# A decoder trunk on one core: the first loads of V's gated weights issued in U's tail, and V's first products formed ahead of U's last chunk

## What is computed

```python
q = (xf @ wq).reshape(n, PEER_HEADS, 2, PEER_DK // 2)
s = jnp.einsum('nhpd,hpkd->nhpk', q, keys)
...                       # top 16 of each head's candidates: experts (128 per row) and gate
hi = jax.nn.gelu(jnp.einsum('bed,bd->be', jnp.take(u_tab, ei, axis=0), xi))
return jnp.einsum('be,bed->bd', gi * hi, jnp.take(v_tab, ei, axis=0))
```

## Time and profile before

| | us |
|---|---|
| median of 3 runs | 3460.92 (3460.67 to 3470.65) |
| the profiled execution, its own time | 3460.77 |
| its span in the trace | 3458.7 |

### The profile page before, as it was taken

One profiled execution on the slowest core, in us unless ns is written; L12 is line 12 of the kernel. 1 busy time (PEld: TensorE's weight loads), 2 busy tenths in 40 slices (PEclk: granted clock), 3 DMA queues, 4 the chain that ended last, 5 costly groups with the idle time before them and its releaser, 6 DMA issues.

```text
span 3458.7 us, 54628 instructions
## 1 busy us (share of the span) xinstructions
PE 3294.1 (95%) x19630; PEld 3118.4 (90%) x19630; DVE 2473.4 (72%) x5134; ACT 1463.5 (42%) x2581; POOL 876.3 (25%) x690
## 2 busy tenths in 40 slices
PE   8998989999999979999998898999999997999998
PEld 7833589999999979999998788999999997999997
DVE  3243268878788868888873327888788877888886
ACT  3222243356666623333333314346666652333333
POOL 3211010000045443334431001000015543343441
PEclk9988999999999989999999879999999998999999
DMA  4254523455599999999972112356569999999994
GB/s 142 97 158 117 160 75 102 141 201 180 204 339 372 364 381 366 360 362 363 361 268 63 48 47 77 105 162 213 180 208 380 382 358 360 369 355 371 355 370 146
DMA packets 315826, 835.34 MB, mean 242 GB/s; under 512 B 32248, under 2 KB 155256, under 8 KB 311440
## 3 DMA queue, kind: packets, MB, share of 16 engines
q1 hardware_dynamic: 233472, 541.63, 44.7%
q0 software_dynamic: 82192, 291.85, 23.2%
HBM read 726.25 MB, written 107.11 MB: 241 GB/s over the span
## 4 chain that ended last, share of the span: by engine, by line
PE 91%; DVE 3%; ACT 2%; DMA 2%; issue 1%; SPq 0%; POOLq 0%; ACTq 0%; POOL 0%; DVEq 0%
PE pstr L1634 30%; PE aux L1711 16%; PE pstr L1711 16%; PE pstr L1423 14%; PE aux L1669 5%; PE pstr L1545 2%; PE pstr L1565 1%; PE aux L1454 1%; PE aux L1463 1%; DMA hl<-hidden 1%; PE aux L1624 1%; PE pstr L1518 1%; PE aux L1765 1%; PE aux L1764 1%; DVE rstd L979 0%
## 5 line engine op out<-in xcount | busy, mean ns | idle before, releaser
L946 DVE TENSOR_TENSOR wlo<-wraw,whi 128x1024 fp32r<-128x1024 f32 x600 | 734.2, 1224 | 589.3 <-ACT whi L680 588.0
L680 ACT ACTIVATE whi<-wraw 128x1024 fp32r<-128x1024 f32 x600 | 632.6, 1055 | 319.8 <-PE pstr L1711 237.5
L1634 PE MATMUL pstr<-xh,whi 128*128 128x392 f32 x2048 | 719.9, 352 | 0.0
L1634 PE MATMUL pstr<-xl,whi 128*128 128x392 f32 x2048 | 699.0, 341 | 0.0
L1634 PE MATMUL pstr<-xh,wlo 128*128 128x392 f32 x2048 | 697.8, 341 | 0.0
L653 POOL DMA_INDIRECT rows<-in_ur,idx x256 | 364.5, 1424 | 1306.2 <-DVE hs L1181 750.8
L653 POOL DMA_INDIRECT rows<-in_v,idx x256 | 378.1, 1477 | 550.1 <-DVE ysum L1194 461.3
L1711 PE MATMUL aux<-wth,whi 128*128 128x392 f32 x1024 | 351.1, 343 | 42.8 <-DVE wtl L1241 42.8
L1634 PEld LDWEIGHTS pstr<-xl,whi 128*128 128x128 f32 x2048 | 386.6, 189 | 0.0
L1634 PEld LDWEIGHTS pstr<-xh,whi 128*128 128x128 f32 x2048 | 386.3, 189 | 0.1
L1634 PEld LDWEIGHTS pstr<-xh,wlo 128*128 128x128 f32 x2048 | 386.2, 189 | 0.0
(11 more groups left out here) (240 smaller groups left out, 5282.0 us busy)
## 6 DMA issues: line engine op xcount, KB each, us to landing
wraw<-in_u SPq DMA_DIRECT2D x256, 512.0 KB, 4.0
wraw<-in_v SPq DMA_DIRECT2D x256, 512.0 KB, 6.4
hidden<-hid SPq DMA_DIRECT2D x256, 196.0 KB, 3.8
gates<-gst SPq DMA_DIRECT2D x28, 1792.0 KB, 9.2
gc<-gates SPq DMA_DIRECT2D x64, 784.0 KB, 10.0
hl<-hidden SPq DMA_DIRECT2D x256, 196.0 KB, 6.6
wraw<-in_w SPq DMA_DIRECT2D x88, 512.0 KB, 3.5
kv<-in_ck SPq DMA_DIRECT2D x32, 256.0 KB, 3.1
```

The costliest lines, as they stand in the source:

```text
L680: e.activation(whi[:, s % RING, :], wraw[:, s % RING, :], ACT.Copy).then_inc(w_hi, 1)
L946: e.tensor_tensor(wlo[:, s % RING, :], wraw[:, s % RING, :], whi[:, s % RING, :].bitcast(F32), ALU.subtract).then_inc(w_lo, 1)
L1634: mm = e.matmul(pstr[:, r % 2, 0, 0:ND], w[:, r, k * P:(k + 1) * P], x[:, k, 0:ND], start=k == 0 and w is whi and x is xh, stop=k == KB - ...
```

## The change

Three things are done.

1. The tiles get other homes. `gc` becomes two tiles that lie over the two buffers of `gst`; `wth` and `wt` lie over the ranking's `tv` and `ti`; `wtl` takes the place over `xt` where `wt` was. None of them lies over the one-hots any more.
2. SyncE issues the first loads inside U's loop: `hl` 0 and 1 behind `store_h(120)`, the first half of the gates behind block 13's store (after a wait for the even blocks), `hl` 2 and 3 behind `store_h(122)`, the second half behind `store_h(123)` (after a wait for the odd blocks, block 13 among them).
3. `gated(0)`, `gated(1)` and `split_wt(0)` on VectorE stand ahead of the split of V's chunk 3 and of the dots of U's chunk 127. `round_wt(0)` on ScalarE stands ahead of `take_hidden(127)`.

No instruction and no transfer is added or taken away.

```diff
-        wt = place("wt", [P, 2, ND], F32, at_xt + 8192)
+        wtl = place("wtl", [P, RING, ND], F32R, at_xt + 8192)
...
+        at_top = used[0]
         tv = place("tv", [P, NT, NPAIR, TOPK], F32)
...
-        used[0] = at_rank
-        gc = place("gc", [P, 2, NB, CPL, SPAN_T], F32)
-        wth = place("wth", [P, RING, ND], F32R)
-        wtl = place("wtl", [P, RING, ND], F32R)
+        gc = [place(f"gc{n}", [P, NB, CPL, SPAN_T], F32, at_gst + n * P * SPAN_T * 4) for n in range(2)]
+        wth = place("wth", [P, RING, ND], F32R, at_top)
+        wt = place("wt", [P, 2, ND], F32, at_top + RING * ND * 4)
...
                             if c == group_slot((b + 1) * BLOCK - 1) + 1:
                                 store_gates(b)
-                for par in range(2):
-                    e.wait_ge(gates_out[par], 16 * (NB // 2) * (layer + 1))
-                load_gates(0, 0)
-                load_gates(0, 1)
-                for c in range(RING):
-                    load_h(c)
+                        if c == G_END - 1:
+                            e.wait_ge(pick_ready, (layer + 1) * (NT - 1))
+                            load_h(0)
+                            load_h(1)
+                        if c == G_END:
+                            e.wait_ge(gates_out[0], 16 * (NB // 2) * (layer + 1))
+                            load_gates(0, 0)
+                        if c == G_END + 1:
+                            load_h(2)
+                            load_h(3)
+                        if c == G_END + 2:
+                            e.wait_ge(gates_out[1], 16 * (NB // 2) * (layer + 1))
+                            load_gates(0, 1)
...
                 for slot in range(N_WQ + N_U):
                     kind, n = mixed(slot)
+                    if slot == N_WQ + N_U - 1:
+                        round_wt(0)
...
-                for c in range(3):
+                for c in range(1, 3):
                     round_wt(c)
...
                 for n in range(MIXED, N_U):
+                    if n == N_U - 1:
+                        gated(0)
+                        gated(1)
+                        split_wt(0)
                     split_next(C_MIX[layer] + table_at(n))
...
-                gated(0)
-                gated(1)
-                split_wt(0)
                 gated(2)
                 split_wt(1)
```

More of the change, by code:

```diff
@@ L350, in trunk @@
         assert used[0] <= at_rank + 8 * N + 8 * NT * P, used[0]
-        used[0] = at_rank
-        gc = place("gc", [P, 2, NB, CPL, SPAN_T], F32)
-        wth = place("wth", [P, RING, ND], F32R)
-        wtl = place("wtl", [P, RING, ND], F32R)
-        assert used[0] <= top, used[0]
+        gc = [place(f"gc{n}", [P, NB, CPL, SPAN_T], F32, at_gst + n * P * SPAN_T * 4) for n in range(2)]
+        wth = place("wth", [P, RING, ND], F32R, at_top)
+        wt = place("wt", [P, 2, ND], F32, at_top + RING * ND * 4)
+        assert (RING + 2) * ND * 4 <= 2 * NT * NPAIR * TOPK * 4
         used[0] = phase
@@ L555, in load_gates @@
                     at = slice(half * (NB // 2), (half + 1) * (NB // 2))
-                    e.dma_start(gc[:, g % 2, at].rearrange("p b c n -> p b (c n)"),
+                    e.dma_start(gc[g % 2][:, at].rearrange("p b c n -> p b (c n)"),
                                 gates[layer][at, :, g * CPL:(g + 1) * CPL, :].rearrange("b p c n -> p b (c n)")).then_inc(g_in[g % 2], 16)
@@ L879, in aside, with round_wt @@
                             rows_gelu(g)
+                def round_wt(c):
+                    e.wait_ge(g_used, layer * N_U + c + 1)
+                    if c >= RING:
+                        e.wait_ge(chunk_done, C_V[layer] + c - RING + 1)
+                    e.activation(wth[:, c % RING, :], wt[:, c % 2, :], ACT.Copy).then_inc(wt_hi, 1)
                 e.wait_ge(out_done, 16 * (5 + layer))
@@ L1215, in one_hots @@
                                         pickt[:, d % 2, 2, r + m:r + m + 1], ALU.is_equal, ALU.mult).then_inc(oh_ready, 1)
[L1217 to L1226, removed]
                 def gated(n):
@@ L1236, in gated @@
                                     hl[:, n % RING, :].rearrange("p (b n) -> p b n", n=SPAN_T),
-                                    gc[:, g % 2, :, n % CPL, :], ALU.mult).then_inc(g_used, 1)
+                                    gc[g % 2][:, :, n % CPL, :], ALU.mult).then_inc(g_used, 1)
                 def split_wt(c):
@@ L1241, in split_wt @@
                     e.tensor_tensor(wtl[:, c % RING, :], wt[:, c % 2, :], wth[:, c % RING, :].bitcast(F32), ALU.subtract).then_inc(wt_lo, 1)
-                gated(0)
-                gated(1)
-                split_wt(0)
+                ranking, ranked = rank_all(), 0
+                next(ranking)
+                for n in range(MIXED, N_U):
+                    if n == N_U - 1:
+                        gated(0)
+                        gated(1)
+                        split_wt(0)
+                    split_next(C_MIX[layer] + table_at(n))
+                    for g in range(groups_by(n + LOOK), groups_by(n + 1 + LOOK)):
+                        one_hots(g)
+                    for _ in range(ranked, RANK_BY[n]):
+                        next(ranking, None)
+                    ranked = RANK_BY[n]
+                    dots(n)
                 gated(2)
```

## The result

| | before | after |
|---|---|---|
| median of 7 runs each, us | 3460.92 (3457.12 to 3470.65) | 3443.95 (3440.86 to 3453.75) |
| ratio after to before, 95% interval | | 0.9945 (0.9927 to 0.9963) |
| the profiled execution, its own time | 3460.77 | 3448.25 |
| its span in the trace | 3458.7 | 3446.2 |

The change makes the kernel 17.0 us faster by the medians, 0.55%; the interval goes from 13 to 25 us. Forecast were 11.6 us and 3449.2: the sign and the range held, the time came out 5.3 us lower, and some of the gain came from a place that the forecast had at nothing.

A forecast was written before the change was run, and what follows sets the result against it. TensorE, busy for 95% of the span, bounds the kernel; only its 42.8 us idle at V's starts could be won. First products 6.2 and 5.4 us sooner: 3460.77 - 11.6 = 3449.2 us, range 3442.0 to 3458.0.

The forecast's parts named there:

- New homes: Moved tiles: sizes and instructions stay, first loads needn't wait for the one-hots' end; cost nothing.
- The landing of the gates: End of U: second half of the gates lands at 1247.6 us in the first layer, 2868.4 in the second.
- the one by bytes: Gates at V's start: 2.38 MB no longer ahead, at 390 GB/s 6.1 us sooner, `gated(0)` at 1247.4 and 2866.5.
- the one by packets: SyncE's queue from block 13's landing: 2560 packets take 28.6 us, so the gates land at 1247.8 and 2870.4.
- VectorE's arrival: VectorE reaching `gated(0)`: unchanged at 1245.68 and 2864.07, 1.9 and 4.3 us ahead of the gates, so not deciding.
- none is needed within some 15 us, so I take nothing for it: SyncE's wait for block 13 in U's tail: V's chunk 3 and stores 124 to 127 queue behind it, at no cost.
- From `gated(0)` to the first product: V's start: 1.8 us stay between `gated(0)` and TensorE's first product, at 1249.4 and 2870.2.
- the bound of 2.8: V's first chunks: at most 2.8 us a layer if both dots wait for rows; bounds 0 and 2.8, taken as 0.
- early gates: Rival at V's start: gates land early, VectorE decides; 8.1 + 9.7 = 17.8 us won, 3443.0; chance 0.17.
- One for one: Rival in U's tail: SyncE's queue gets only the gathers' 80 packets a us; 2.6 us won, 3458.2; chance 0.22.
- SyncE's queue clogs: Rival in U's tail: gates' 1792 runs hold up V's chunks 1 to 3; slower, 3475 us; chance 0.05.
- my three marks for being wrong: First products before 1246 or after 1253; VectorE's row waits growing over 4 us; TensorE waits inside V's first chunks.

The follow-up runs named there:

- e1: Kernel before with only the new homes of gc, wth, wtl and wt, loads and order as before: 3457.62 us, ratio 0.9985 to before.
- e2: Changed kernel with VectorE and ScalarE back in the order of before, new homes and early loads kept: 3457.48 us, ratio 0.9987 to before.
- e8: Changed kernel fetching 256 bytes a row, not 4 KB, in U's last 13 gathers; read by trace alone, stands 5.43 and 7.30 us.
- e3: Changed kernel with at most one dot in each of U's chunks from 119 on, 92 dots in U: 3413.25 us, ratio 0.9857 to before.

## Where the prediction went wrong, and where it held

*New homes: "Cost nothing".* This is the step that failed, and it makes most of the difference: V's pass became 4.3 us faster, as the trace of e1 shows. I priced the move as if only waits could change and set no bound on the pace of the products. The forecast of 3449.2 less these 4.3 is 3444.9, beside a measured 3443.95. That it comes so near is partly luck: 2.8 us too little at the turns and 1.9 us of waits inside V, which I had at nothing, nearly cancel.

*The landing of the gates.* Counted from U's end, the second half was to land at 1247.6 - 1235.2 = 12.4 and 2868.4 - 2853.2 = 15.2 us. It landed at 1229.04 + 20.6 - 1239.59 = 10.0 and at 13.4 us (2862.78), some 2 us sooner in both layers. Of the two counts, the one by bytes (12.2 and 13.3 us behind U's end) was right in the second layer, the one by packets (12.6 and 17.2) in neither. The count by packets had 2560 packets in 28.6 us; from block 13's landing at 1225.85 to the half's landing at 1249.65 the queues passed, after (packets, MB, share):

```profile
q0 software_dynamic: 1498, 5.47, 57.1%
q1 hardware_dynamic: 2837, 4.04, 46.6%
```

That is 2837 of SyncE's in 23.8 us, 119 a us, where the sum has 90 in the mean.

*VectorE's arrival: unchanged, does not decide.* Counted the same way it was to come 10.5 and 10.9 us behind U's end and came 11.2 and, less the wait of 3.03 us for the gates, 10.35 behind it. The size was right, but since the gates landed sooner it does decide in the first layer. The reason is not the dots' waits for rows: those were 7.2 us in 8 waits and 8.8 in 8, below. It is V's chunk 2, whose load landed late; the waits in the first layer (1205 to 1253), then in the second (2815 to 2865):

```profile
DVE rows L1190 <- DMA rows<-in_ur,idx: 7.2, 8, 2.9
DVE wlo L955 <- ACT whi L687: 5.1, 3, 2.4
...
DVE rows L1190 <- DMA rows<-in_ur,idx: 8.8, 8, 2.6
DVE wt L1233 <- DMA gc<-gates: 3.0, 1, 3.0
DVE wlo L955 <- ACT whi L687: 2.7, 2, 2.4
```

*SyncE: "none is needed within some 15 us, so I take nothing for it".* Wrong as a mechanism. I looked for waits on semaphores and found them short, but the issues themselves took up to 11.70 us, and V's chunks 1 to 3 landed 20.5 to 22.0 us behind their issue, where they had needed 6.4 to 10.1. SyncE came to the second half of the gates at 1229.0, not at 1218.9; 4.4 of these 10.1 us are U's later end. The trace before had a sign of it that the earlier trace rows leave out, since they end ahead of it: four issues, right behind the same two halves of the gates, that took 9.02 us together.

```profile
1237.51 9.02 SPq L550 DMA_DIRECT2D hl<-hidden  x4
```

e2 shows the price: with VectorE in its old order the late chunk 3 eats the whole gain of the early loads. That the changed kernel does not pay it lies in its new order, which sets chunk 3 behind `gated(0)`. I let the order bring VectorE to `gated(0)` ahead of the gates and counted what it pushes back, but nothing in the sum says what the early loads are worth without it: by e2 next to nothing.

*From `gated(0)` to the first product*: 1.8 us forecast, 1.94 and 1.87 measured. *The sum of the turns*: 11.6 forecast, 14.4 measured.

*V's first chunks: no wait.* Right in the second layer; 1.9 us in the first, inside the bound of 2.8 but for another reason. Not the dots but the load of V's chunk 5 was late: issued at 1254.25, it landed 15.1 us later, the split behind it began at 1270.43 after a wait of 6.06 us for ScalarE, and `split_wt(4)`, which TensorE wanted at 1271.6, stands behind that split.

*The rivals.* The time of "early gates" (3443.0) is the nearest to the measured one, yet its mechanism is not what happened: it has VectorE decide in both layers and all 17.8 us come from the turns. "One for one" is out: the rows above have 2837 packets of SyncE's beside 1498 of the gathers, 119 a us, where that rival has 80. "SyncE's queue clogs" was real in the chunk loads, but by the same 119 not past its turning point of 75 packets a us in the first layer. Of my three marks for being wrong, only TensorE's waits inside V's first chunks came up; the first products counted from U's end lie 13.15 and 15.25 us behind it, against 14.2 and 17.0.

## What to carry to other kernels

Where two latecomers end within a few us of each other, removing either alone shows nothing, and an experiment on one half proves little: loads alone and order alone brought 1.6 and 2.7 us, no more than the scatter, both together 15.3. A load that is issued early goes ahead of the others in its queue; list all that stands behind it, and when the DMA engines are already full, first take bytes out (13 of 105 dots moved into V brought some 30 us on top of the change's 17). And a tile that moves may change the pace of the engine that reads it, so count the instructions in a steady stretch, not only the waits.

## What the runs showed of the hardware that was not expected

- The pace of TensorE's products depends on the addresses of the tiles: 472.24, 471.84, 470.59 and 470.41 us for the same 110 chunks, at the full granted clock, with no idle time and the same instructions, each number repeated in both layers to 0.01 us. The Trainium skill, page "SBUF — State Buffer", section "Who interferes with whom", says that PE and ACT never wait on anyone. The measurement, 0.39% between the slowest and the fastest placing of the tiles, shows that something in the placing holds TensorE up; whether that is a wait on another engine's access, and which, no run here shows.
- An issue on SyncE took 10 to 12 us instead of 0.33 (11.70 and 10.37 us for the load of V's chunk 3 in the changed kernel, 10.12 in e2). It did so with two halves of the gates in short runs of 896 bytes ahead of it in the queue and full DMA engines; in the first layer it took 0.93 us with thin rows (e8) and 3.54 with fewer dots (e3).
- The stand of 1.38 us left the granted clock at 1.00; the stands of 5.43 us and more ended with a first product of 0.66 or 0.67 us, at the lower of the clock's two levels, and a first chunk of 5.8 to 7.2 us in place of 4.3.
